# Gathering expert 0's tokens straight from x in float32, with the norm factor in the selection

## What is computed

```
h = rms_norm(x, g_pre_ffn) * (1 + sc2) + sh2        # x: 256 x 1024, the residual after the mixer
logits = h @ w_router + b_router                     # 32 experts
top_v, top_i = top_k(logits, 4); gates = softmax(top_v)
for each expert e, for the tokens that chose it:
    u = h[tokens] @ w_mlp1[e] + b_mlp1[e]            # 1024 x 2048, float32
    a = clipped SwiGLU(u)
    out[tokens] += gate * (a @ w_mlp2[e] + b_mlp2[e])   # 1024 x 1024
x = x + gt2 * rms_norm(out, g_post_ffn)
```

## Time and profile before

| | us |
|---|---|
| timed runs | 1652.22, 1652.75, 1655.72 (median 1652.75) |
| profiled execution, its device time | 1651.91 |
| its span, first to last instruction | 1650.2 |
| first block up to the gather | 0 to 163 |
| experts | 163 to 1094 |
| second block | from there |

### The profile page before, as it was taken

How to read it: one execution, slowest core, us unless ns; L and a number is a source line. 1 busy time by engine, 2 the same in 40 slices (tenths; PEclk the granted TensorE clock), 3 DMA queues, 4 the chain that set the end, 5 groups by cost and what they waited for, 6 DMA issues and landing times.

```text
span 1650.2 us, 25076 instructions
## 1 busy us (share of the span) xinstructions
PE 1574.9 (95%) x10535; PEld 966.5 (59%) x10535; DVE 649.4 (39%) x1090; ACT 427.3 (26%) x729; POOL 155.7 (9%) x251
## 2 busy tenths in 40 slices
PE   6999999999999998899999999999999999999998
PEld 4777333343443333333343433359999899999997
DVE  3577221121121121112121212147666776876665
ACT  2555010010000000000010000045444545544444
POOL 1120111011101110101110111000000131000000
PEclk9999999999999999999999999999999999999999
DMA  9988999999999999999999999985446543535450
GB/s 397 353 309 330 390 420 374 415 429 426 429 425 428 428 426 428 406 425 429 427 428 427 428 426 428 423 330 195 189 179 236 201 157 128 205 131 199 182 192 27
DMA packets 54574, 544.65 MB, mean 330 GB/s; under 512 B 6257, under 2 KB 6385, under 8 KB 7985
## 3 DMA queue, kind: packets, MB, share of 16 engines
q1 hardware_dynamic: 54304, 542.62, 80.4%
q10 hardware_dynamic: 144, 0.26, 0.0%
HBM read 541.81 MB, written 1.05 MB: 329 GB/s over the span
## 4 chain that ended last, share of the span: by engine, by line
PE 51%; DMA 4%; DVE 2%; ACT 1%; issue 0%; DVEq 0%
PE bank L1051 10%; PE bank L1280 7%; PE bank L1286 7%; PE bank L1283 7%; PE bank L1098 5%; DMA w<-in_w_mlp 4%; PE bank L1298 3%; PE bank L1301 3%; PE bank L1295 3%; PE bank L1019 1%; PE bank L982 0%; DVE lin L1963 0%; DVE lin L1958 0%; DVE lin L1954 0%; PE bank L968 0%
## 5 line engine op out<-in xcount | busy, mean ns | idle before, releaser
L1051 PE MATMUL bank<-w,xT 128*64 128x512 f32 x2048 | 471.9, 614 | 10.9 <-DMA w<-in_w_mlp 10.9
L1051 PEld LDWEIGHTS bank<-w,xT 128*64 128x64 f32 x2048 | 154.5, 135 | 309.1 <-issue 278.8
L1280 PE MATMUL bank<-nh,Wh 128*128 128x256 f32 x912 | 258.1, 283 | 0.5 <-DVE nl L2044 0.5
L1286 PE MATMUL bank<-nl,Wh 128*128 128x256 f32 x912 | 256.5, 281 | 0.0
L1283 PE MATMUL bank<-nh,Wl 128*128 128x256 f32 x912 | 256.1, 281 | 0.0
L1098 PE MATMUL bank<-w,aT 128*64 128x512 f32 x1024 | 227.4, 595 | 7.7 <-ACT aT L2592 5.2
L1992 DVE TENSOR_TENSOR Wl<-w,Wh 128x1024 fp32r<-128x1024 f32 x176 | 209.3, 1230 | 51.5 <-ACT Wh L2627 51.5
L1950 DVE TENSOR_SCALAR glu<-bank 128x512 f32<-128x512 f32 x32 | 22.1, 691 | 461.0 <-PE bank L1051 419.1
L2627 ACT ACTIVATE Wh<-w 128x1024 fp32r<-128x1024 f32 x184 | 184.6, 1053 | 17.3 <-PE bank L1301 14.5
L1280 PEld LDWEIGHTS bank<-nh,Wh 128*128 128x128 f32 x912 | 171.7, 188 | 4.8 <-issue 1.7
L1283 PEld LDWEIGHTS bank<-nh,Wl 128*128 128x128 f32 x912 | 171.9, 188 | 1.8
(11 more groups left out here) (453 smaller groups left out, 1743.5 us busy)
## 6 DMA issues: line engine op xcount, KB each, us to landing
w<-in_w_mlp SPq DMA_DIRECT2D x150, 2048.0 KB, 24.5
w<-in_w_mlp SPq DMA_DIRECT2D x83, 1024.0 KB, 11.6
w<-in_w_ada SPq DMA_DIRECT2D x24, 1024.0 KB, 10.4
w<-in_ffn_w_gate SPq DMA_DIRECT2D x22, 1024.0 KB, 4.9
w<-in_ffn_w_up SPq DMA_DIRECT2D x22, 1024.0 KB, 7.0
w<-in_ffn_w_down SPq DMA_DIRECT2D x22, 1024.0 KB, 4.8
w<-in_w_in SPq DMA_DIRECT2D x9, 1024.0 KB, 17.0
w<-in_w_out SPq DMA_DIRECT2D x8, 1024.0 KB, 4.9
```

Of the source, the lines that this page charges most:

```text
L1051: mm = pe.matmul(Ub[half(j), :], xT[e % 2][:, kt % 2 * 4 + kt // 2, :], w[:, 1024 * j + o:1024 * j + 1024:2], start=False, stop=(kt == 7), ...
L1280: pe.matmul(o, wh_[:, k, :], h[:, k, :], start=(k == 0), stop=False)
L1286: mm = pe.matmul(o, wh_[:, k, :], l[:, k, :], start=False, stop=(k == nk - 1))
```

## The change

For expert 0 alone, the three-term gather is replaced. VectorE makes, in place of `Sb[0]`, a float32 selection `S0r`, which holds each token's norm factor where `Sb` held a 1: two instructions, one for each token tile, since the factor is a number per token. TensorE multiplies the new x itself (float32, its columns with a step of two elements, `parity(t)`) with it: 8 blocks x 2 tiles = 16 float32 matmuls in place of 48 in bfloat16. The second tile's three VectorE steps towards the terms (`part(1, 0)` ahead of `pos`, `part(1, 1)`, `part_low(0)` and `part_low(1)` behind the counts) move behind `scaled` of expert 0 and ahead of the gates; the gather of expert 1 is now the first that needs the terms, and waits for them. The four bias matmuls of expert 0 move from behind the counts to between the first tile's count and the wait for the second tile's `mkb`.

```diff
+        S0r = at("S0r", SC + 6656, [2, 64])
...
             pe.matmul(bank[6][:, 0:32], stri, mkb[:, 0, :], start=True, stop=True)
+            expert_bias(pe, 0)
             pe.wait_ge(*route_v("hot", 1))
...
+            def gather_first(B, k0, k1):
+                for kt in range(k0, k1):
+                    for t in range(2):
+                        mm = pe.matmul(B[:, 64 * (kt - k0):64 * (kt - k0) + 64], parity(t)[:, kt // 4, 128 * (kt % 4):128 * (kt % 4) + 128],
+                                       S0r[:, t, :], start=(kt == k0 and t == 0), stop=(kt == k1 - 1 and t == 1),
+                                       skip_group_check=True)
                 return mm
...
                 if e == 0:
-                    pe.wait_ge(*part_s("hi", 1))
                     pe.wait_ge(*route_v("S"))
-                    gather_part(0, M, 0, 4).then_inc(*gath_p.hit("first"))
+                    gather_first(M, 0, 4).then_inc(*gath_p.hit("first"))
                     pe.wait_ge(*route_v("cnt"))
-                    gather_part(0, Y, 4, 8).then_inc(*gath_p.hit(0))
+                    gather_first(Y, 4, 8).then_inc(*gath_p.hit(0))
                     return
                 pe.wait_ge(*S_g(e))
+                if e == 1:
+                    for c in range(2):
+                        pe.wait_ge(*part_s("mid", 1, c))
+                    pe.wait_ge(*part_g("lo", 0))
+                    pe.wait_ge(*route_v("lo", 1, 1))
...
-            bias(0)
             gather(0)
...
-            part(1, 0, 1, 0)
             v.wait_ge(*route_p("cnt"))
...
-            v.tensor_tensor(Sb[0], iota64.unsqueeze(1).to_broadcast([128, 2, 64]),
-                            pos[:, :, 0:1].to_broadcast([128, 2, 64]), A.is_equal).then_inc(*route_v.hit("S"))
+            for t in range(2):
+                i = v.tensor_scalar(S0r[:, t, :], iota64, pos[:, t, 0:1], ss[:, 14 + t:15 + t], A.is_equal, A.mult)
+            i.then_inc(*route_v.hit("S"))
             v.tensor_copy(cnt, bank[6][:, 64:96]).then_inc(*route_v.hit("cnt"))
-            part(1, 1, 1, 1)
-            part_low(0)
-            part_low(1)
...
             scaled("first", 0, M, 0, 4)
             scaled(0, 0, Y, 4, 8)
+            last_terms()
```

More of the change, by code:

```diff
@@ L463, in build @@
         route_v = sig("route_v", "zb", ("part", 0), ("lb", 0), ("lg", 0), ("max", 0), ("idx", 0), ("eq", 0), ("hot", 0),
[L464 to L465 removed]
+                      ("lb", 1), ("lg", 1), ("max", 1), ("idx", 1), ("eq", 1), ("hot", 1), "pos", "S",
+                      "cnt", ("part", 1, 0), ("part", 1, 1), ("lo", 1, 0), ("lo", 1, 1))
         gates_v = sig("gates_v", "sub", "sum", "rec", "mul", ("m4", 0), ("m4", 1), "G")
@@ L564, in build, with expert_bias @@
         pair = [(bank[0], bank[1]), (bank[2], bank[3])]
+        def expert_bias(pe, e):
+            if e == 0:
+                pe.wait_ge(*const_v("sel"))
+                pe.wait_ge(*b1_g("s", 1))
+                pe.wait_ge(*b1_s("lo", 1))
+                pe.wait_ge(*route_v("lg", 1))
+            else:
+                pe.wait_ge(*aT_s(e - 1, 1))
+            for Ub, o in ((UG, 0), (UL, 1)):
+                for j in range(2):
+                    pe.matmul(Ub[half(j), :], sel[:, e:e + 1].to_broadcast([96, 64]),
+                              b1[:, 1024 * j + o:1024 * j + 1024:2], start=True, stop=False,
+                              skip_group_check=True, tile_position=(0, 64 * j))
         def pe_first(pe):
@@ L958, in bias @@
             def bias(e):
[L959 to L984, removed]
+                expert_bias(pe, e)
+            def gather_first(B, k0, k1):
[4 more added lines that the diff above has]
+                                       skip_group_check=True)
                 return mm
@@ L999, in gather @@
                     pe.wait_ge(*xTm_v(e - 1))
-                gather_part(e, M, 0, 8).then_inc(*gath_p.hit(e))
+                todo = [(kt, p, t) for kt in range(8) for p in range(3) for t in range(2)]
+                for n, (kt, p, t) in enumerate(todo):
+                    mm = pe.matmul(M[:, 64 * kt:64 * kt + 64], xb[:, p, t, 128 * kt:128 * kt + 128], Sb[e % 2][:, t, :],
+                                   start=(n == 0), stop=(n == len(todo) - 1), skip_group_check=True)
+                mm.then_inc(*gath_p.hit(e))
             def gates(p):
@@ L1881, in dve_first, with last_terms, dve_moe @@
             v.wait_ge(*route_v("pos"))
-            v.tensor_tensor(Sb[0], iota64.unsqueeze(1).to_broadcast([128, 2, 64]),
-                            pos[:, :, 0:1].to_broadcast([128, 2, 64]), A.is_equal).then_inc(*route_v.hit("S"))
+            for t in range(2):
+                i = v.tensor_scalar(S0r[:, t, :], iota64, pos[:, t, 0:1], ss[:, 14 + t:15 + t], A.is_equal, A.mult)
+            i.then_inc(*route_v.hit("S"))
             v.tensor_copy(cnt, bank[6][:, 64:96]).then_inc(*route_v.hit("cnt"))
-            part(1, 1, 1, 1)
-            part_low(0)
-            part_low(1)
-        def dve_moe(v):
+            def last_terms():
+                for i in range(2):
+                    part(1, i, 1, i)
+                for i in range(2):
+                    part_low(i)
+            return last_terms
+        def dve_moe(v, last_terms):
             x_registers(v, "dve")
```

7 lines of the change are left out of this document (5 added, 2 removed).

## The result

The changed kernel took 1659.14 us in the median of 9 runs (1653.75 to 1660.79), the kernel before 1652.75 in 9 runs beside it (1651.45 to 1656.94). The ratio is 1.0034, with a 95% interval of 1.0025 to 1.0043: 6.4 us slower, where 0.5 us faster had been forecast and 1654.9 was the upper end of the range.

The account below looks back on a forecast made before the run. TensorE was taken to bound the kernel up to 286 us, the loads afterwards. Between 0.25 us lost at low clock and 1.25 gained at full, 0.5 was taken: 1652.75 - 0.5 = 1652.2 us, range 1649.7 to 1654.9.

Parts of the forecast that it names:

- What bounds the kernel: In the experts, TensorE sets when loads go on up to 286 us; afterwards the loads set when TensorE goes on.
- from 286 on the loads run without a break: In the experts, DMA loads were claimed to have no further dry place after 281 to 286 us (share 1.00).
- reach the end in full: Any gain at expert 0's gather was claimed to arrive whole at the kernel's end, if below 3.3 us.
- pos, selection, bias, start of the gather: Ahead of expert 0's gather: pos 0.2 us earlier, selection 0.4, bias fits before 161.81; gather starts 0.27 us earlier.
- The gather: Expert 0's float32 gather: gemm1(0) starts 0.25 us later at low clock, 1.25 us earlier at full clock.
- Sixteen: 1.8 us at 2.4 GHz: Expert 0's gather priced as sixteen float32 loads: 1.8 us at full clock, 3.6 us at half.
- the 5.1 us for the old gather: Estimate for expert 0's old gather from a load rule: 48 x 0.107 us, making the change gain 3.4 us there.
- (b): Rival at expert 0's gather: slower float32 loads at low clock, 1.95 us lost, 1654.7; chance 0.20, 0.03 for doubled price.
- Moved terms and gates: Behind expert 0's gather, 3.0 us of VectorE terms ahead of the gates would fit in idle time and cost nothing.
- Rival (a): At the routing and expert 0's gather the clock stays up: 2.5 us gained, 1650.2; chance 0.20.
- Rival (c): Loads set the gap at 281 us, so an earlier gemm1 ends waiting and nothing arrives: 1652.75; chance 0.05.

Follow-up runs that it names:

- e2: The changed kernel with expert 0's four bias matmuls back behind the counts; 1659.07 us, ratio 1.0033 to the kernel before.
- e7: The kernel before with fifteen spare matmuls (30 pairs) between expert 0's gather and gemm1(0), delaying gemm1(0); 1659.60 us, ratio 1.0040.
- e5: The kernel before with four spare matmuls in TensorE's idle time ahead of expert 0's gather; 1653.92 us, ratio 1.0008.
- e6: The kernel before with expert 0's bias moved as in the change and four spare matmuls in TensorE's idle time; 1654.13 us, ratio 1.0007.
- e8: The changed kernel with expert 0's gather as 16 bfloat16 matmuls of the high term alone, middle and low left out; 1653.59 us, ratio 0.9998.
- e9: The changed kernel with expert 0's gather as 16 bfloat16 high-term matmuls, each issued twice (32 pairs); 1652.99 us, ratio 1.0000.
- e4: The changed kernel with five spare matmuls in TensorE's idle time ahead of expert 0's gather; 1651.88 us, ratio 0.9993 to the kernel before.
- e3: The changed kernel with expert 0's float32 gather over the first token tile alone, 8 matmuls; 1654.98 us, ratio 1.0011 to the kernel before.
- e10: The kernel before with three spare matmuls between the first tile's count and the wait for the second mkb; 1652.94 us, ratio 1.0001.
- e1: The kernel before with only expert 0's four bias matmuls moved ahead of the wait for the second mkb; 1652.75 us, ratio 1.0002.

## Why the prediction was wrong

**What bounds the kernel: right for a loss, not borne out for a gain.** The lateness of gemm1(0) passed through the dry places of the DMA engines and to the end, as the chain and the stretches had been read (after, e2, e7). But "from 286 on the loads run without a break" was wrong: the row that it names ends at 400, and at 695 to 710 there is a third dry place. The bytes that the DMA engines had moved by a given time tell most directly where after fell behind: taken over 427 GB/s, what it lacked of them against before was worth -0.3 us at 160 us, 4.1 at 200, 6.2 at 305 and 6.0 at 680, 8.1 at 720 and 8.3 at 1000. So it falls behind at each of the three dry places and hardly between them. And "reach the end in full" isn't seen the other way: e5 and e6 ended gemm1(0) 1.2 us earlier, and a gain of 1.2 lies outside both intervals; e8 and e9 ended it 1.7 and 1.9 us earlier, and no median shows it. The profiled execution of e9 has a span 3.7 us shorter than that of before, but it is the fastest of its twelve (1648.24 us).

**pos, selection, bias, start of the gather: nearly right.** pos started 0.04 us behind the last count's end (161.80), the bias was over by 161.13, the selection took 0.54 where I had 0.4 and 0.5 at worst. The gather began 1.18 us behind the first count of the second tile, against 1.31 before and 1.04 forecast: half of the 0.27 us that I had put down. All counts were 0.3 us earlier than before already, by the shift.

**The gather: the step that failed.** It was the term "Sixteen: 1.8 us at 2.4 GHz", "3.6 us" at half. The price of a pair was right: 0.12 us at full clock (3.98/32 in e4) against my 0.11 to 0.13, 0.22 at half (7.09/32) against my 0.22. The number of pairs was wrong by two: a float32 matmul as the program lists it is issued as two pairs. The trace of before showed it. The order lists `four,lb` once for each tile, and its row has an x2 for one tile and an x4 for both the earlier trace rows; I took the x2 for two matmuls of the program. What made it easy to miss is the row beside it: `ident,lin` has an x2 too, and there the program lists two (L1079, transposes by TensorE), so a float32 transpose is one pair and a float32 matmul two. gemm1(0) itself shows it as well: its loops at L1051 list 8 x 2 x 2 = 32 matmuls, not the 64 that I gave for it ahead of the prediction; 64 is the trace's count. Two places of the trace of before would have settled it, this one among them; the other is TensorE's timeline at the up-projection's scatter, four listed float32 matmuls of 512 columns:

```profile
304.58 3.70 PE L1019 MATMUL bank<-ysb,SGT 128*128 128x512 f32 x8
```

3.70 us for four is 0.93 each. In the second block the program declares the operands of the same shape as float32r; the trace prints them as f32 too, but has each listed matmul once, 0.23 us apart:

```profile
1484.07 0.39 PE L1295 MATMUL bank<-Wh,ah 128*128 128x512 f32 x1
1484.30 0.40 PE L1298 MATMUL bank<-Wl,ah 128*128 128x512 f32 x1
```

So a float32 matmul takes four times one of these. The Trainium skill has this in "FP8 and Floating Point Precision", section "TensorE Precision Notes": true float32 takes four passes through the array. By this it would be two pairs of two passes each, and the trace agrees with it in the time (0.93 against 4 x 0.23) and in the two pairs; the passes within a pair no trace shows. From the measured start, 32 pairs at half clock give 162.69 + 7.09 = 169.8 for gemm1's start, where 169.70 was measured.

What the prediction set against its rows as a rule of the Trainium skill ("TensorE: Matmul & The Clock Gate", section "LDWEIGHTS (loading the stationary operand)") was read too widely: the section gives the number of columns over 1.2 GHz and doesn't say "whatever the type", so the 5.1 us for the old gather was my own step. No sum and no chance used it. The range's upper end was added up wrongly too: half a microsecond beyond (b) is 1655.2, not 1654.9; the result lies above either.

**The rival that came true.** That was (b) in the form that I gave 0.03: "at 0.42 us each ... gemm1 would start 3.4 us late, and only that would be seen as slower". A listed matmul cost 0.44 and gemm1 started 3.5 us late (3.8 counted from the first count). I had asked whether strided reads double the price and never whether the count did. The other half of (b), that the clock comes back later, came as well: 13.7 us low in place of 6.8, which made gemm1(0) 1.25 us longer than before. Together that is 4.7 us at the end of gemm1(0) (186.82 against 182.08), 5.0 counted from the first count, and 1652.75 + 5.0 = 1657.8 is what a right sum would have given. That a strided read would have doubled the price, the reason that I had given for it, is not shown: the pair's price was as forecast with the stride.

**What was open behind gemm1(0).** After lost 4.1 to 7.1 us by the ratio's interval and e2 3.5 to 7.3, e3 0.2 to 3.6; with gemm1(0) 5.0, 3.7 and 0.5 us late, none of them asks for more. e7 does (4.2 late, 4.6 to 8.4 lost), and so do the gains that don't arrive. TensorE's timeline shows what they share. In an extra pass it has to gather 48 small matmuls (`Sx`). "issue" marks idle time in which the engine waited for nothing that the profile shows. The second extra pass in before, then in after and in e8, then the first in e7:

```profile
651.26 1.35 PE L1113 MATMUL bank<-Sx,xb 128*128 128x32 bf16 x48 [1.84 <-issue]
662.85 1.31 PE L1125 MATMUL bank<-Sx,xb 128*128 128x32 bf16 x43 [5.20 <-issue]
655.92 0.90 PE L1126 MATMUL bank<-Sx,xb 128*128 128x32 bf16 x27 [4.82 <-issue]
252.71 0.46 PE L1115 MATMUL bank<-Sx,xb 128*128 128x32 bf16 x11 [4.35 <-issue]
```

In after TensorE halts for 5.20 us behind 5 of the 48, in e8 for 4.82 behind 21. The place moves with the length of TensorE's own list. After, e2 and e9 have 32 pairs in expert 0's gather and halt behind 5; e3 and e8 have 16 pairs there, 16 fewer, and halt behind 21, 16 later. In the first extra pass the same sum holds: e7, with 30 pairs more than before, halts behind 37 pairs of the pass; e5 and e6, with 8 more, behind 59; e10, with 6 more, behind 61; before itself behind 67, each time 67 less what was added. Where it falls among the small matmuls of `Sx` it costs 4.4 to 5.5 us, among the longer ones behind them 0.5 to 1.7. In the first pass of e1, e4, after and the other kernels made from it none is seen, nor in the second of those made from before. What TensorE waits for at this place no run shows.

The six profiles in which it falls into `Sx` (after, e2, e3, e8, e9 in the second extra pass, e7 in the first) are also the only ones with a low clock for 10.2 us in an extra pass. By the bytes, the first five fell behind by 1.0 to 3.2 us more at the third dry place (after 2.1), where the other profiles gained up to 1.1 or stayed; e7 fell behind by 2.5 between 240 and 270. That is of the size of what was missing: e7's 4.2 + 2.5 = 6.7 against 6.6 measured, e3's 0.5 + 1.3 = 1.8 against 1.8, and in e8 2.6 stands against the gain of 1.7. So some 2 us of after's loss may be the price not of the float32 gather itself but of where this halt fell. Each kernel has one profile, and no run moved the halt alone, so its share in the medians isn't shown. Still open is after's lag at the second dry place (2.1 us, with the clock low at 250.0 to 256.8 and 284.1 to 287.5, where in before it wasn't), and why the gains of e5 and e6 don't reach their medians.

**Moved terms and gates: right.** VectorE did the terms from 170.61 to 173.4, GpSimd had Sb of expert 1 at 178.7, 8 us ahead of its reader at 186.75, which waited for nothing; VectorE idled for 10.5 us before its next task, where it had idled for 12.0. Only the hour was off, 4 us later, with gemm1. **Rival (a)**, the clock stays up: not so; it fell 0.8 us earlier (161.2). **Rival (c)**, nothing arrives: refuted by e7 for a delay; for a gain no run refutes it.

## What to carry to other kernels

Price a float32 matmul by the pairs that the trace shows for it, not by the lines of the program: divide a row's count by the count in the instruction list before multiplying. Here one float32 matmul of 64 columns cost as much as eight bfloat16 ones at half clock (0.44 against 0.055) and at full (0.25 against 0.03), so three exact bfloat16 terms were cheaper than one float32 term, though they are three times as many. Where a gather stands ahead of the first use of a ring of loads, a delay of some microseconds reached the end in full (after, e2, e7). And before two profiles are subtracted, count from an instruction that both kernels reach with the same list, and look behind the change for idle time that moved: changing the number of one engine's instructions at 163 us moved a halt of 5 us at 657 us.

## What the runs showed of the hardware

- **Two pairs for a float32 matmul.** 16 listed are 32 pairs (after), 8 are 16 (e3), 15 are 30 (e7), and gemm1(0)'s 32 are 64. A float32 transpose (L1079) and a float32r matmul (L1298) are one. A pair with a 128x128 load and 64 columns took 0.22 us at 1.2 GHz and 0.12 at 2.4.
- **A halt at a fixed place in TensorE's list.** It came one pair earlier in the extra pass for each pair added ahead of it (67, 61, 59, 37 in before, e10, e5 and e6, e7) and cost 0.5 to 5.5 us by what stood there.
- **Weight loads slow with the clock.** The load of float32 128x128 took 331 ns in the median of after's gather at half clock, 188 at full; in e4's gather, the same loads at full clock, 196.
- **Spare matmuls kept the clock up.** In the profiles of e4, e5, e6 and e10 it stayed at 1.00 through the gather, after TensorE had been busy for 3.33 to 3.74 of the 4 us up to 162.00; in before and after it had been busy for 2.38 and 2.77, and fell. In all eight kernels without spare matmuls ahead of the gather it fell, between 161.2 and 164.7. e1 and e8 were busy for 3.3 us there as well, and their clock fell at 164.2 and 164.7, so the busy time up to 162.00 alone doesn't tell.
- **The clock doesn't fall at the same places in like stretches.** At 240 to 260, where TensorE's list is the same in all these kernels, the clock was at 1.00 in before, e2, e3, e6 and e9 and low for 3.4 us in e4, 6.8 in after, e1, e5, e8 and e10 and 10.2 in e7. Over the span it was low for 17 us in before's profile and for 54 in that of after. A difference of a few microseconds between two profiles is no more than that until the place of each low spell has been compared.
